# Pairing the gate units of the stick-breaking attention at every second step

## The reference

```python
def stick_breaking_attention(q, k, v):
    ...
        z = jnp.einsum('bhqd,bhkd->bhqk', q[:, :, s0:s1], k[:, :, :s1]).astype(jnp.float32) * scale
        mask = (s0 + jnp.arange(BLOCK))[:, None] > jnp.arange(s1)[None, :]
        log_beta = jax.nn.log_sigmoid(z)
        log_1m = jnp.where(mask, jax.nn.log_sigmoid(-z), 0.0)
        suffix = lax.cumsum(log_1m, axis=3, reverse=True) - log_1m
        a = jnp.exp(jnp.where(mask, log_beta + suffix, -jnp.inf))
        outs.append(jnp.einsum('bhqk,bhkd->bhqd', a.astype(v.dtype), v[:, :, :s1]))
    ...
            o = stick_breaking_attention(q, k_sb, v_sb).transpose(0, 2, 1, 3).reshape(B, S, SB_W)
            om = memory_attention(qm, mem, i, mem_norm, mem_w_kv, mem_q_norm, mem_k_norm)
            y = jnp.concatenate([o, om], axis=-1) * jax.nn.silu(gate)
            x = x + y @ b_w_out[j]
```

## Time and profile before

| | |
|---|---|
| median of 3 runs | 2304.29 us (2301.74 to 2306.15) |
| the profiled execution | 2306.71 us, its span 2304.9 us |
| mean granted TensorE clock | 0.984 |
| TensorE busy | 2209.3 us, 96% |
| VectorE busy | 1173.9 us, 51% |
| GpSimd busy | 1142.7 us, 50% |
| ScalarE busy | 930.8 us, 40% |

### The profile page before, as it was taken

One profiled execution on the slowest core, in us unless ns is written; L12 is line 12 of the kernel. 1 busy time (PEld: TensorE's weight loads), 2 busy tenths in 40 slices (PEclk: granted clock), 3 DMA queues, 4 the chain that ended last, 5 costly groups with the idle time before them and its releaser, 6 DMA issues.

```text
span 2304.9 us, 27404 instructions
## 1 busy us (share of the span) xinstructions
PE 2209.3 (96%) x10006; PEld 1699.9 (74%) x10006; DVE 1173.9 (51%) x1816; ACT 930.8 (40%) x1583; POOL 1142.7 (50%) x1360
## 2 busy tenths in 40 slices
PE   7999989999899999999999999799999999999999
PEld 5776567765577668888887788576678888877786
DVE  6877865458656341043248744464420342298542
ACT  4546642356425553232234622344532322237322
POOL 3553235642146224565466666353145665575752
PEclk9999999999999999999999999899999999999999
DMA  3222122311123113332332233122133333332321
GB/s 144 79 82 68 37 65 92 110 65 38 37 82 100 47 46 119 108 93 90 89 97 92 83 102 100 55 84 64 37 110 92 96 97 89 94 101 74 110 92 64
DMA packets 53126, 191.45 MB, mean 83 GB/s; under 512 B 6016, under 2 KB 6400, under 8 KB 52480
## 3 DMA queue, kind: packets, MB, share of 16 engines
q1 hardware_dynamic: 51696, 184.44, 25.8%
q10 hardware_dynamic: 1296, 5.24, 0.6%
HBM read 187.56 MB, written 2.10 MB: 82 GB/s over the span
## 4 chain that ended last, share of the span: by engine, by line
PE 78%; DVE 13%; ACT 4%; POOL 2%; issue 2%; DMA 1%; SPq 0%; DVEq 0%; ACTq 0%
PE proj L552 20%; PE proj L553 19%; PE proj L554 19%; PE score L548 5%; PE proj L548 4%; PE stat L548 2%; PE turned L548 2%; POOL lower L504 2%; PE mix L548 2%; DVE small L1781 2%; PE score L553 1%; PE score L552 1%; PE score L554 1%; PE ptp L801 1%; DVE prob L1770 1%
## 5 line engine op out<-in xcount | busy, mean ns | idle before, releaser
L504 POOL TENSOR_TENSOR lower<-raw_ring,upper 128x256 fp32r<-128x256 f32 x1340 | 1126.6, 874 | 1107.3 <-ACT upper L1198 1106.9
L552 PE MATMUL proj<-h,upper 128*128 128x512 f32 x1440 | 582.7, 405 | 12.1 <-ACT sq L1296 3.2
L1198 ACT ACTIVATE upper<-raw_ring 128x1024 fp32r<-128x1024 f32 x335 | 350.8, 1058 | 551.9 <-PE proj L552 293.7
L554 PE MATMUL proj<-h,lower 128*128 128x512 f32 x1440 | 562.8, 391 | 0.0
L553 PE MATMUL proj<-h,upper 128*128 128x512 f32 x1440 | 562.5, 391 | 0.0
L552 PEld LDWEIGHTS proj<-h,upper 128*128 128x128 f32 x1440 | 271.3, 188 | 78.1 <-issue 5.9
L554 PEld LDWEIGHTS proj<-h,lower 128*128 128x128 f32 x1440 | 271.1, 188 | 57.9
L553 PEld LDWEIGHTS proj<-h,upper 128*128 128x128 f32 x1440 | 271.8, 189 | 51.8 <-issue 1.9
L552 PE MATMUL proj<-y,upper 128*128 128x512 f32 x586 | 234.7, 400 | 13.8 <-ACT qk L1296 5.7
L554 PE MATMUL proj<-y,lower 128*128 128x512 f32 x586 | 229.7, 392 | 0.0
L553 PE MATMUL proj<-y,upper 128*128 128x512 f32 x586 | 229.6, 392 | 0.0
(11 more groups left out here) (446 smaller groups left out, 3416.5 us busy)
## 6 DMA issues: line engine op xcount, KB each, us to landing
raw_ring<-stream SPq DMA_DIRECT2D x335, 512.0 KB, 3.6
landing<-stream SPq DMA_DIRECT2D x5, 512.0 KB, 9.3
x<-x_in SPq DMA_DIRECT2D x4, 512.0 KB, 6.1
rows<-rows_in ACTq DMA_DIRECT2D x2, 1024.0 KB, 5.3
out<-x SPq DMA_DIRECT2D x8, 256.0 KB, 2.0
memraw<-mem_in SPq DMA_DIRECT2D x1, 1024.0 KB, 12.7
memraw<-mem_in ACTq DMA_DIRECT2D x1, 1024.0 KB, 5.0
rot<-tables_in ACTq DMA_DIRECT2D x2, 512.0 KB, 3.6
```

The source lines that it names most:

```text
L504: ins = nc.gpsimd.tensor_tensor(lower[:, p % RING, a:b], slot_source(p)[:, a:b], upper[:, p % RING, a:b].bitcast(FP32), ALU.subtract)
L552: first_ = nc.tensor.matmul(o, lhsT[0], rhs[0], start=start, stop=False)
L554: return first_, nc.tensor.matmul(o, lhsT[1], rhs[0], start=False, stop=stop)
L1198: nc.scalar.activation(upper[:, p % RING, :], slot_source(p), ACT.Copy).then_inc(split_upper, 1)
```

## The change

One expression in `gate_units` is changed:

```diff
--- before.py
+++ after.py
@@ -451,7 +451,7 @@
         if kind == "mla":
             return sum(n for n, _ in BESIDE_LATENT[:z + 1])
         if kind == "stick":
-            return min(z + 1 + min(max(z - 39, 0), 3), 8 * MT)
+            return min(2 * ((z + 1) // 2) + min(max(z - 39, 0), 3), 8 * MT)
         if kind == "diff":
             return 2 * (z + 1)
         return min(z + 1, 14)
```

## The result

| | before | after |
|---|---|---|
| median of 8 runs each, side by side | 2304.76 us (2301.74 to 2306.34) | 2311.55 us (2308.90 to 2312.52) |
| ratio, 95% interval | | 1.0028 [1.0017, 1.0039] |
| profiled execution, its span | 2306.71, 2304.9 | 2310.74, 2308.9 |
| mean granted clock in it | 0.984 | 0.985 |

The account below looks back on a forecast made before the run. TensorE was taken as the bound almost everywhere, VectorE close behind. Terms -1.0 + 0.65 + 4.2 + 1.9 = +5.8 us gave 2312.5 for the profiled execution, 2310.1 on the median; range 2303.3 to 2316.0.

Parts of the forecast that it names:

- The mechanism: Tiles 2 to 4: later first unit frees the weight slot later, so ScalarE's copy L1198 holds step 4's sigmoids; +1.4 us each.
- the rival in which the sigmoids are not held: Tiles 2 to 4: slot already free at L1198, about 0 us each; sum +1.5, 2305.8 us; chance 0.20.
- Tile 0: First attention tile: scores replace the unit that waited 0.58 for ScalarE's read of the last queries; -1.0 us.
- Tile 1: Second attention tile: VectorE bounds it, and two units instead of one follow transposition 7; +0.65 us.
- Tiles 2 to 4: Attention tiles: held sigmoids delay step 4's scan and `prob` 7, then two units follow transposition 7; +1.4 us each, +4.2.
- the term for contention: Tiles 2 to 4: some 0.5 us more GpSimd work beside VectorE's costs +0.25 us, between 0 and 0.35.
- the three waits that I named: TensorE waits of 0.5 to 1 us before transpositions 5, 6 and 7, the one before 7 new.
- Crossing: Tile 5 into the memory part: last gate's sigmoid falls between exps of steps 48 and 49, two more table loads; +1.9 us.
- dearer crossing: Rival, crossing: ScalarE stops beyond each load (2.3 us), or TensorE stays longer at half clock (2.5); sum +8.3, 2312.6; chance 0.12.
- The clock: Crossing: clock already at half (0.50) from 585 to 590 us before the change; same stretch assumed again, a little later.
- Neighbours and restarts: TensorE units behind other units save 0.09 us each after transpositions; taken as 0, ends 0 and -2.2 us.

Follow-up runs that it names:

- pair at step 7 only: Kernel before with only the unit of a tile's step 6 moved behind transposition 7, tiles 0 to 4; one timing, 2310.45 us beside 2306.82.
- The two single pieces: Kernel before with only step 0's unit moved to step 1, or only step 6's to step 7, tiles 0 to 4: 2306.94 and 2310.45 us beside 2306.82.
- last tile only: Units as before up to step 39, the last tile's units as in the change: 2309.19 us, 1.0016 of before.
- the copy later: The change with ScalarE's weight slot copy of a tile's step 0 taken one step later, behind step 4's sigmoids: 2310.19 us, 1.0020 of before.

## Why the prediction was right, and where its terms were off

Forecast 2310.1, from 2303.3 to 2316.0, slower at 0.61: measured 2311.55. The mechanism is the one named, and the rival in which the sigmoids are not held fell with the first row of L1198. But the sum, +5.8 for 6.8, hides errors of both signs, and that it came so near is in part luck: tile 0 brought 0.75 less than forecast, tiles 1 to 4 cost 1.2 less, and 1.5 for the clock (against before at full clock) was not in the sum. The sum was also made against an execution of before with `mix` at half clock; against that one the stage grew by 4.6, not 5.8. One sum in the text is wrong: the upper bounds listed for the terms add up to 7.8 (-0.6 + 0.8 + 4.8 + 2.8), not 9.0. By the same working the top of the range would be 2314.6, and the measured time lies below that too.

- **Tile 0: -1.0, measured -0.25.** The wait of 0.58 for the queries went as said. What was overlooked stands one step later: ahead of the first unit there is now transposition 1, and by the trace it waited 0.33 for the `pt` copy of step 0 (L1350), which ScalarE makes only after the queries' copy and two sigmoids. The 0.58 less this 0.33 is the gain measured. VectorE's idle of 1.19, which I gave a part of the gain, was no part of TensorE's path: TensorE is busy for 11.87 of 12.20 us. TensorE after, tile 0:

```profile
494.79 0.30 PE L801 MATMUL stat<-const,prob 128*128 128x128 f32 x1 [0.33 <-ACT pt L1350]
494.93 0.47 PE L552 MATMUL proj<-h,upper 128*128 128x512 f32 x1
```

- **Tile 1: +0.65, measured +0.49.** As said, the second unit behind transposition 7; that this is all of it, "pair at step 7 only" shows.
- **Tiles 2 to 4: +1.4 each, measured +1.04, 1.07 and 1.06.** The steps came at +3.51 (unit), +4.08 (copy), +5.05 (sigmoid) and +5.62 (scan), forecast +3.60, +4.20, +5.15 and +5.75: 0.13 early by the end. The other 0.22 is the term for contention, the slowing of VectorE and GpSimd beside each other. I had VectorE pay 0.25 more for 0.5 us more of overlap, at the rate of the earlier trace rows. The overlap grew by 1.0, and VectorE's chain from this scan to `prob` 7 took 8.40 us against 8.37; GpSimd paid, 4.42 for 3.94. Of the three waits that I named, the one before transposition 6 did not come: transposition 5 waits 0.88 in its place, and behind it 6 finds `prob` ready.
- **Crossing: +1.9, measured +1.87.** The exp of step 48 at +14.29 in its tile (forecast +14.34), the sigmoid at +16.17 (+16.19), `mix` at +19.67 (+19.69). VectorE's L1959 did stand ahead of the maximum of step 49, and was hidden by the table load beside it. The next instruction starts 1.30 us after each load's start, at 584.11 and 586.51 alike. The Trainium skill, "ScalarE: Activation LUTs", section "What ACT_TABLE_LOAD costs", adds a drain of about 1380 ns to each load of 1283 ns; the load agrees with the row, and of the drain these rows show nothing. The dearer crossing's first half, a stop beyond the load at each switch, thus did not come.
- **The clock: 0, measured +1.5 against before's two executions at full clock, -0.6 against the one at half (3.89 for 4.53).** This is the step that failed. The forecast read one execution of before, found `mix` at 0.50 and took that for before's state. It was one of two. By the means of before's three executions and the change's two (3.09 and 3.83 us) the term is +0.7; how often each state comes in the timed executions stays open. The dearer crossing's second half, a longer stay at half clock, is not what the traces show: `mix` took 3.6 to 3.95 us behind 4.5 us of waiting, and 3.7 to 4.5 behind 1.96 where the clock fell.
- **Neighbours and restarts: 0, as taken.** The two single pieces leave nothing over for them in tiles 2 to 4.

## What to carry to other kernels

Before a producer is moved behind other work, look at what the engine that waits for it has queued up: here a copy of a weight slot, itself never urgent, stood on ScalarE ahead of the sigmoids that the critical loop needed. Work moved behind the last step of a loop in which another engine sets the pace adds nearly all of itself to the turn-round: here 0.61 of a unit's 0.69 us when nothing else moved. And before a difference of 0.2% is costed from one trace, read the clock of the same stretch in a second and a third one.

## What the runs showed of the hardware that was not expected

- The same kernel, with tile lengths equal to 0.02 us, had a product of sixteen matmuls once in 4.53 us and twice in 2.37, by the granted clock (0.50 and 1.00), behind the same idle time of 1.96 us. With 0.24 of idle it was at full clock both times, with 4.5 at half for most of it all four times. In the change the clock read 0.99 over the whole stretch up to `mix`, TensorE's idle 4.5 us included, and 0.50 in the next 2 us; in "last tile only" it was down already while TensorE did nothing. Four idle us of the change, then of "last tile only":

```profile
584.00:588.00 4.00, 0.00 (x0) 0.00 (x0) 1.76 (x5) 3.94 (x7) 0.00 (x0) 1.00 0.00 0
```

```profile
582.00:586.00 4.00, 0.00 (x0) 0.00 (x0) 1.79 (x6) 3.94 (x6) 0.00 (x0) 0.65 0.00 0
```

- VectorE and GpSimd slow each other at no fixed rate. Four subtractions took 3.94 us in before, 4.42 in the change and 4.96 with the copy later, as more of them lay beside VectorE's scans and multiplications; the same chain on VectorE took 8.37, 8.40 and 8.64.
